# Two-layer conditioned decoder trunk: forming the first four conditioning pieces with TensorE, ahead of the layer that uses them

## The chip, the cores and the metric

The kernel runs on one core of one Trainium2 chip. The metric is the device time of one execution in microseconds; the kernel before and the changed kernel compute the same outputs from the same inputs.

## What is computed

Two layers, each a token mixer and a routed mixture of experts, on 512 tokens of 1024 features in f32. A vector `c` of 1024 numbers conditions each layer: `silu(c)` times a matrix of 1024 x 6144 plus a bias gives six rows of 1024, and the layer uses them as shift, scale and gate of its two halves.

```python
def reference(x, c, positions, w_ada, b_ada, ...):
    cond = jax.nn.silu(c)
    for l in range(DEPTH):                                    # DEPTH = 2
        mod = (cond @ w_ada[l] + b_ada[l])[:, None, :]        # 6 x 1024
        shift1, scale1, gate1, shift2, scale2, gate2 = jnp.split(mod, 6, axis=-1)
        h = _ada_norm(x, shift1, scale1)                      # rms(x) * (1 + scale1) + shift1
        x = x + gate1 * _token_mixer(h, positions, w_in[l], ...)
        h = _ada_norm(x, shift2, scale2)
        x = x + gate2 * _moe(h, w_router[l], ...)             # 64 experts, 8 per token
    return _rms_norm(x, final_gain)
```

`mod` is formed in twelve pieces of 512 columns. Pieces 0 and 1 are shift1, 2 and 3 are scale1: the first thing that a layer needs.

## The kernel before

`trunk` (from line 146) writes an opening block, a loop `Fori(0, DEPTH)` whose body is `mixer` and `experts`, each one block with a program for every engine and a barrier behind it, and a closing block with the last norm. Inside a block each engine runs its own list in the order in which it is written, held by semaphores. SP issues nearly all transfers, one after the other from one list, so a transfer is also held by every wait that stands before it in SP's list.

**Opening block (lines 196 to 245).** SP loads positions, the constants and x (2 MB). VectorE and ScalarE form the rotary tables (the last one at line 244), ScalarE the squares of x (line 238) and the root. TensorE has nothing there.

**Start of the mixer.** SP loads c, then eight blocks of 1 MB of `w_ada` (`ada`, line 388) and four short bias rows, then the input weights `w_in` in two parts (line 402: 1664 KB with the columns of queries and keys, then 3072 KB) and small weights. ScalarE applies silu to c (line 452). VectorE forms pieces 0 to 3 (lines 592 and 594): for each of eight chunks of 128 features it multiplies the 128 x 512 block by the chunk's column of c and adds, 32 operations. TensorE sums over the partitions with a matmul of ones (line 737), ScalarE copies the piece into `mod` (line 457). Then VectorE forms the normalised rows `h`, four tiles of 128 tokens, with lines 607 and 608; two tiles are in flight, and the third waits for TensorE's transposes (line 746) of the first.

The input projection works with split operands: every f32 operand is a rounded part ("hi") and a remainder ("lo"), and a product is three matmuls at the rate of the rounded type. So in front of it ScalarE rounds w_in chunk by chunk (line 461), GpSimd forms the remainders of the first part (line 437) after two small edits for the rotary columns (lines 433, 434), and VectorE forms those of the transposed rows (line 614) and of the second part (line 624). The rounded chunks 0 and 1 lie where `mod` keeps shift1 and scale1, so they come last, after line 608. TensorE's first product (line 753) waits for all eight remainders of GpSimd:

```python
pe.wait_ge(s_in_lo[0], DC)
pe.wait_ge(s_hT_hi, TJ)
```

The attention then runs head by head, and pieces 4 to 11 are formed beside it in the same way, one per head.

**Experts and combine.** Experts run in groups of three steps: two experts with split operands ("one") and a pair in plain f32 ("two"; lines 1719 and 1738). Each step gathers its tokens' rows and scatters its result to `y_rows` in HBM with indirect transfers that GpSimd issues (line 1241). SP's list brings the weights (lines 1130 to 1155). When all scatters have landed, SP reads `y_rows` back in 16 parts of 1 MB (line 1196, four buffers in `raw_gu`), VectorE adds them up tile by tile and adds the gated sum to x (lines 1592 to 1598), and ScalarE squares each finished tile (line 1365) and takes the root (line 1367) for the next norm. TensorE has nothing to do in the combine. The four tiles are one loop on each engine:

```python
for u in range(4 * TJ):
    wait(sp, s_ysum, u - 3)
    sp.dma_start(y_part[u % 4], y_rows[:, 2 * (u % 4):2 * (u % 4) + 2, u // 4, :]).then_inc(y_in[u % 4], 16)
```

## Time and profile before

| | |
|---|---|
| median of 3 runs | 2301.84 us (2300.92 to 2304.58) |
| the profiled execution | 2307.99 us, its span 2306.2 us |
| TensorE matmul busy | 1887.9 us, 82% of the span |
| VectorE busy | 1305.5 us, 57% |
| ScalarE, GpSimd busy | 914.2 us, 375.9 us |
| moved | 619.39 MB, mean 269 GB/s |
| mean granted TensorE clock | 0.891 |

The page gives busy time by engine and by group of instructions, with the idle time ahead of each and what ended it. A line number is a line of the kernel. PE is TensorE's matmul, PEld its loading of the stationary operand, DVE is VectorE, ACT ScalarE, POOL GpSimd, SP the engine that issues transfers; SPq is its queue. The two layers start their mixers at 22.58 and 1134.06 us.

### The profile page before, as it was taken

To read this page: it belongs to the slowest core of one execution; us is meant where nothing else is said; L and a number is where in the kernel's file an instruction comes from. 1 tells how busy PE (TensorE), PEld (TensorE's weight loads), DVE (VectorE), ACT (ScalarE), POOL (GpSimd) and SP (SyncE) were. 2 spreads that over 40 slices of the span, in tenths; PEclk is the share of its full clock that TensorE was granted. 3 is DMA by queue.
4 is the path that set the end of the run, shared out by engine and by line. 5 is a ranking of instruction groups with operands and counts; after the bars stand their busy time and mean duration, and the time that the engine had idled before them with its cause. 6 is when DMAs were issued, how large, how long until landed. Compare 5 with 4: busy or idle time off the path is not lost. (4 is left out here: it accounts for less than half of the span.)

```text
span 2306.2 us, 31250 instructions
## 1 busy us (share of the span) xinstructions
PE 1887.9 (82%) x8864; PEld 1313.8 (57%) x8865; DVE 1305.5 (57%) x1982; ACT 914.2 (40%) x1340; POOL 375.9 (16%) x281
## 2 busy tenths in 40 slices
PE   1888889889999899994068888988899989999960
PEld 0655677666666666662046456856666656666640
DVE  5647636555554546463774782556655554646447
ACT  2324521454544545451122342136454544545431
POOL 0200300122212222110020021002122212222110
PEclk9998889999989999997569779888899989999985
DMA  7035233689999999995632530556799999999956
GB/s 288 22 121 186 74 122 146 235 348 400 392 374 363 370 357 376 377 367 204 259 139 69 199 111 1 201 223 251 307 386 398 382 371 349 382 358 370 371 219 276
DMA packets 135180, 619.39 MB, mean 269 GB/s; under 512 B 22744, under 2 KB 25816, under 8 KB 81904
## 3 DMA queue, kind: packets, MB, share of 16 engines
q1 hardware_dynamic: 112240, 550.62, 62.8%
q0 software_dynamic: 22784, 67.13, 8.2%
q8 instruction: 44, 0.72, 0.1%
q14 instruction: 112, 0.92, 0.1%
HBM read 584.14 MB, written 46.14 MB: 273 GB/s over the span
## 5 line engine op out<-in xcount | busy, mean ns | idle before, releaser
L1526 DVE TENSOR_TENSOR w_lod<-raw_d,w_hid 128x2048 fp32r<-128x2048 f32 x72 | 165.4, 2297 | 263.2 <-ACT w_hid L1302 263.2
L1227 POOL DMA_INDIRECT mixT<-h_rows,gidx x104 | 144.9, 1393 | 787.4 <-issue 583.9
L1719 PE MATMUL bank<-hT,hbT 128*64 128x512 f32 x512 | 226.6, 595 | 0.0
L1719 PE MATMUL bank<-mod,hbT 128*64 128x512 f32 x512 | 226.6, 595 | 0.0
L1241 POOL DMA_INDIRECT y_rows<-mixT,sidx x104 | 144.5, 1390 | 459.8 <-issue 371.3
L1317 ACT ACTIVATE mixT<-bank 128x512 f32<-128x512 f32 x208 | 113.1, 600 | 208.2 <-PE bank L1738 116.3
L1685 PEld LDWEIGHTS bank<-meta,mod 128*128 128x128 f32 x1088 | 139.2, 198 | 66.8 <-issue 62.4
L1523 DVE TENSOR_TENSOR w_loa<-raw_gu,w_hia 128x2048 fp32r<-128x2048 f32 x72 | 164.8, 2290 | 19.8 <-ACT w_hia L1299 19.8
L1523 DVE TENSOR_TENSOR w_lob<-raw_gu,w_hib 128x2048 fp32r<-128x2048 f32 x72 | 164.4, 2283 | 0.0
L1342 ACT ACTIVATE mod<-bank 128x256 f32<-128x256 f32 x104 | 39.6, 381 | 309.5 <-PE bank L1698 178.0
L1685 PE MATMUL bank<-meta,mod 128*128 x1088 | 137.8, 254 | 29.8 <-DVE mod L1502 29.8
L1302 ACT ACTIVATE w_hid<-raw_d 128x2048 fp32r<-128x2048 f32 x72 | 138.1, 1917 | 37.3 <-DMA raw_d<-in_w_down 37.2
L1738 PE MATMUL bank<-h,actT 128*64 128x512 f32 x256 | 147.5, 730 | 5.4 <-ACT mixT L1317 5.4
L737 PE MATMUL bank<-acc,const 128*128 128x512 f32 x48 | 35.8, 838 | 141.1 <-DVE acc L594 141.1
L1299 ACT ACTIVATE w_hia<-raw_gu 128x2048 fp32r<-128x2048 f32 x72 | 137.6, 1911 | 29.6 <-PE bank L1698 29.5
L1692 PE MATMUL bank<-const,mixT 128*128 128x128 f32 x832 | 132.2, 309 | 20.6 <-POOLq L1235 20.5
L1696 PE MATMUL bank<-w_hia,hbT_r 128*128 128x512 f32 x288 | 124.3, 432 | 29.0 <-DVE hbT_lo L1531 25.6
L1738 PE MATMUL bank<-raw_d,actT 128*64 128x512 f32 x256 | 147.6, 730 | 0.0
L1719 PEld LDWEIGHTS bank<-hT,hbT 128*64 128x64 f32 x512 | 67.5, 137 | 131.8 <-issue 127.9
L1516 DVE COPY listed<-bank 128x3 f32 (+3 forms) x136 | 21.8, 160 | 205.2 <-PE bank L1685 204.1
L1299 ACT ACTIVATE w_hib<-raw_gu 128x2048 fp32r<-128x2048 f32 x72 | 137.9, 1915 | 0.0
L1692 PEld LDWEIGHTS bank<-const,mixT 128*128 128x128 f32 x832 | 118.1, 206 | 23.5 <-POOLq L1235 22.3
(347 smaller groups left out, 4228.4 us busy)
## 6 DMA issues: line engine op xcount, KB each, us to landing
raw_d<-in_w_down SPq DMA_DIRECT2D x104, 1024.0 KB, 11.1
raw_gu<-in_w_gate SPq DMA_DIRECT2D x72, 1024.0 KB, 10.9
raw_gu<-in_w_up SPq DMA_DIRECT2D x72, 1024.0 KB, 17.3
w_ada_sb<-in_w_ada SPq DMA_DIRECT2D x40, 1024.0 KB, 5.7
hT<-in_w_gate SPq DMA_DIRECT2D x32, 1024.0 KB, 7.9
hT<-in_w_up SPq DMA_DIRECT2D x32, 1024.0 KB, 13.3
mod<-in_w_gate SPq DMA_DIRECT2D x32, 1024.0 KB, 12.8
mod<-in_w_up SPq DMA_DIRECT2D x32, 1024.0 KB, 17.4
```

The lines of the kernel that those rows point to most:

```text
L1227: by_rows(s, lambda rows: pool.indirect_dma_start(out=hb[s.par][0:rows], out_offset=None, in_=h2_dram, in_offset=bass.IndirectOffsetOnAxis ...
L1241: by_rows(s, lambda rows: pool.indirect_dma_start(out=y_dram, in_=yb[s.par][0:rows], in_offset=None, out_offset=bass.IndirectOffsetOnAxis( ...
L1299: act.activation(w_hi[k][:].rearrange("p c g f -> p g c f"), raw_gu[s.side][:, :, 4 * k:4 * k + 4, :], ACT.Copy).then_inc(hi[k], 1)
L1302: act.activation(w_hi[2][:], raw_d[s.down_at][:], ACT.Copy).then_inc(hi[2], 1)
L1317: i = act.activation(yb[s.par][:, 512 * b:512 * b + 512], bank_y[b][:], ACT.Copy)
L1523: dve.tensor_tensor(w_lo[k][:].rearrange("p c g f -> p g c f"), raw_gu[s.side][:, :, 4 * k:4 * k + 4, :], w_hi[k][:].bitcast(F32).rearrang ...
L1526: dve.tensor_tensor(w_lo[2][:], raw_d[s.down_at][:], w_hi[2][:].bitcast(F32), ALU.subtract).then_inc(lo[2], 1)
L1685: i = pe.matmul(bank_l[:, 3 * k:3 * k + 3], sel[:, j, :], meta[:, j, bass.ds(e, 1), :].rearrange("p e k -> p (e k)"), start=j == 0, stop=j ...
L1692: i = pe.transpose(bank_t[c // 4][:, (c % 4) * P:(c % 4) * P + P], hb[s.par][:, c:D:DC], ident)
L1696: pe.matmul(dst, a_hi, b_hi, start=first, stop=False)
L1719: i = pe.matmul(bank_g[s.par][lane, :], hbT[:, c, lane], pair_gu[k][:, :, c, :], start=c == 0, stop=c == DC - 1)
L1738: i = pe.matmul(bank_y[b][lane, :], actT[:, c, lane], pair_d[k][:, c, 512 * b:512 * b + 512], start=c == 0, stop=c == 1)
```

## The change

- The opening block also loads c, the first layer's bias row (4 x 512) and its first 8 MB of w_ada, as four transfers of 2 MB (two chunks of 128 features, 2048 columns each) with x between the first and the second. ScalarE applies silu to c once into `cond`, which stays for the whole program.
- `first_pieces` lets TensorE do the whole product: the stationary operand is one column of `cond` repeated 128 times, the moving operand 512 columns of w_ada, so each output row is the product, and the result stands in all 128 partitions. Four banks hold pieces 0 to 3, eight chunks are summed in them, and the bias comes as a ninth product of a row of ones with the bias row: 36 matmuls in plain f32. `first_out` lets ScalarE copy the four banks to `mod`.
- The mixer no longer forms pieces 0 to 3. SP starts with w_in, VectorE with the normalisation.
- At the end of the experts of the first layer (`l < DEPTH - 1`, a branch on SP, ACT and PE) SP loads the next layer's first 8 MB of w_ada in eight pieces of 1 MB and the bias row, into weight buffers that the last steps leave free, each pair after the wait that says so; TensorE runs `first_pieces` behind its last down product, ScalarE `first_out` ahead of its squares of the combine.
- The parts of y_rows are read into the buffers of the split weights (`w_hi`, `w_lo`) instead of `raw_gu`.

The diff, cut to its core:

```diff
@@ trunk
+        cond = sb("cond", [P, DC])
...
+        def first_pieces(pe, w, row, arrived, done):
+
+            for c in range(DC):
+                pe.wait_ge(arrived[c], 16)
+                for q in range(4):
+                    pe.matmul(bank[q][:], cond[:, c:c + 1].to_broadcast([P, P]), w[c][:, q * 512:q * 512 + 512], start=c == 0, stop=False)
+            for q in range(4):
+                pe.matmul(bank[q][:], ones[0:1, :], row[:, q * 512:q * 512 + 512], start=False, stop=True).then_inc(done, 1)
+
+        def first_out(act, done):
+
+            for q in range(4):
+                act.wait_ge(done, q + 1)
+                i = act.activation(mod[:, q // 2, (q % 2) * 512:(q % 2) * 512 + 512], bank[q][:], ACT.Copy, bias=1.0 if q // 2 == SCALE1 else 0.0)
+            return i
...
                 sp.dma_start(const[:], ins["const"]).then_inc(s_start, 16)
-                sp.dma_start(x[:], x_in.rearrange("o (j p) n -> p (o j) n", p=P)).then_inc(s_x_in, 16)
+                sp.dma_start(raw_cond[:], c_in.rearrange("o (p c) -> p (o c)", c=DC)).then_inc(s_cond, 16)
+                sp.dma_start(first_row[:], ins["b_ada"][0:1, 0:4 * 512]).then_inc(d_first[0], 16)
+                src = ins["w_ada"][0:1].rearrange("o (p c) n -> p (o c) n", c=DC)
+                for i in range(4):
+                    sp.dma_start(first_w[:, 2 * i:2 * i + 2, :], src[:, 2 * i:2 * i + 2, 0:4 * 512]).then_inc(d_first[i], 16)
+                    if i == 0:
+                        sp.dma_start(x[:], x_in.rearrange("o (j p) n -> p (o j) n", p=P)).then_inc(s_x_in, 16)
...
+            @block.tensor
+            def _(pe):
+                pe.wait_ge(s_start, 32)
+                pe.wait_ge(s_cond, 17)
+                pe.wait_ge(d_first[0], 32)
+                first_pieces(pe, [first_w[:, c, :] for c in range(DC)], first_row, [d_first[c // 2] for c in range(DC)], s_first)
...
+                act.wait_ge(s_cond, 16)
+                act.activation(cond[:], raw_cond[:], ACT.Silu).then_inc(s_cond, 1)
...
                 act.wait_ge(s_start, 32 + 4 + 16)
+                first_out(act, s_first).then_inc(s_cond, 1)
+                act.wait_ge(s_cond, 18)
@@ mixer, SP
-                sp.dma_start(cond[:, 0, :], ins["c"].rearrange("o (p c) -> p (o c)", c=DC)).then_inc(d_small, 16)
-                ada(0)
-                sp.wait_ge(s_blank, 1)
-                for q in range(4):
-                    ada_row(q)
-                for u in range(1, 8):
-                    ada(u)
@@ mixer, ACT
-                for q in range(4):
-                    mod_out(q)
                 act.wait_ge(s_rot, 1)
-                act.wait_ge(s_unit, 8)
@@ mixer, DVE
-                for q in range(4):
-                    ada(q)
                 link(dve.reciprocal(stat[:, 8:12], stat[:, 20:24]))
-                dve.wait_ge(s_mod, 4)
@@ mixer, PE
-                for q in range(4):
-                    ada(q)
@@ experts
+        y_part = [plain[:].rearrange("p c g f -> p (c g f)").rearrange("p (k n) -> p k n", k=2) for plain, _ in both_hi + both_lo]
+        room = [raw_gu[0][:].rearrange("p g c f -> p (g c f)"), raw_gu[1][:].rearrange("p g c f -> p (g c f)"), hT[:].rearrange("p a n -> p (a n)")]
+        coming = [r[:, i * 2048:i * 2048 + 2048] for r in room for i in range(2)] + [plain[:].rearrange("p c n -> p (c n)") for plain in (hi_d, lo_d)]
+        coming_row = raw_d[0][0:1].rearrange("p a n -> p (a n)")
@@ experts, SP
+                last = group(GROUPS - 1, half + 1, 1)
+                with sp.If(l < DEPTH - 1):
...
+                    for i in range(2):
+                        sp.wait_ge(lo[1], last[i].order + 1)
+                        piece(2 * i)
+                        piece(2 * i + 1)
+                    sp.wait_ge(lo[2], last[1].order + 1)
+                    sp.dma_start(coming_row, ins["b_ada"][DEPTH - 1:DEPTH, 0:4 * 512]).then_inc(d_coming_row, 16)
+                    sp.wait_ge(s_gu, last[2].n + 1)
+                    piece(4)
+                    piece(5)
+                    sp.wait_ge(s_down, last[1].n + 1)
+                    piece(6)
+                    piece(7)
                 sp.wait_ge(s_scattered, (more + 3 * (GROUPS // 2)) * 2 + 2)
@@ experts, ACT
                 steps(act, step)
+                with act.If(l < DEPTH - 1):
+                    v["first_out"](act, s_first).then_inc(s_moved, 1)
+                    act.wait_ge(s_moved, 1)
@@ experts, PE
                 steps(pe, step)
+                with pe.If(l < DEPTH - 1):
+                    pe.wait_ge(d_coming_row, 16)
+                    v["first_pieces"](pe, coming, coming_row, d_coming, s_first)
```

How instructions move, as the two programs are built (a row is a line, an operation, what it writes from what, its shape and how many follow one another; the changed kernel's lines are numbered anew). First VectorE from the start of the mixer, before:

```order
L592 SCALAR_TENSOR_TENSOR acc<-w_ada_sb,cond,b_ada_rows 128x512
L594 SCALAR_TENSOR_TENSOR acc<-w_ada_sb,cond,acc 128x512 x7
L592 SCALAR_TENSOR_TENSOR acc<-hT,cond,b_ada_rows 128x512
L594 SCALAR_TENSOR_TENSOR acc<-hT,cond,acc 128x512 x7
L592 SCALAR_TENSOR_TENSOR acc<-mixT,cond,b_ada_rows 128x512
L594 SCALAR_TENSOR_TENSOR acc<-mixT,cond,acc 128x512 x7
L603 RECIPROCAL stat<-stat 128x4
L607 SCALAR_TENSOR_TENSOR h<-x,stat,mod 128x1024
```

and changed, where the normalisation is the first thing in the block:

```order
L586 UNCONDITIONAL_BRANCH
L615 RECIPROCAL stat<-stat 128x4
L618 SCALAR_TENSOR_TENSOR h<-x,stat,mod 128x1024
L619 TENSOR_TENSOR h<-h,mod 128x1024
L625 TENSOR_TENSOR hT_r<-bank,w_uq_sb_r 128x4x128
```

Then TensorE at the end of the experts' block in the changed kernel, where before the branch out of the block followed the last down product directly:

```order
L1776 MATMUL bank<-h,actT 64x512
L1776 MATMUL bank<-raw_d,actT 64x512
L1810 COMPARE_AND_BRANCH
L203 MATMUL bank<-raw_gu,cond 128x512 x16
L203 MATMUL bank<-hT,cond 128x512 x8
L203 MATMUL bank<-w_hid,cond 128x512 x4
L203 MATMUL bank<-w_lod,cond 128x512 x4
L205 MATMUL bank<-raw_d,const 128x512 x4
```

and SP at the same place, behind the last transfers of expert weights and ahead of the first read of y_rows:

```order
L1171 DMA raw_d<-in_w_down 128x2048
L1210 COMPARE_AND_BRANCH
L1214 DMA raw_gu<-in_w_ada 128x2048 x2
L1221 DMA raw_d<-in_b_ada 1x2048
L1214 DMA hT<-in_w_ada 128x2048 x2
L1214 DMA w_hid<-in_w_ada 128x2048
L1214 DMA w_lod<-in_w_ada 128x2048
L1231 DMA w_hia<-y_rows 128x2x1024
```

Nine transfers that were the next block's first now stand in this list between the weights and the parts of y_rows.

## Rows read from the trace of the kernel before

**Rows 1.** The page's groups of instructions: busy, mean ns, idle before, releaser.

```profile
L737 PE MATMUL bank<-acc,const 128*128 128x512 f32 x48 | 35.8, 838 | 141.1 <-DVE acc L594 141.1
```

**Rows 2.** Timeline of the first layer's start: start us, duration, instruction.

```profile
22.58 1.28 ACT L452 ACT_TABLE_LOAD   x1 [0.50 <-PEq L197]
...
23.17 0.41 SPq L388 DMA_DIRECT2D w_ada_sb<-in_w_ada  x1
...
28.45 0.75 DVE L592 SCALAR_TENSOR_TENSOR acc<-w_ada_sb,cond,b_ada_rows 128x512 f32<-128x512 f32 x1 [10.66 <-DMA w_ada_sb<-in_w_ada]
...
52.32 0.65 POOL L433 TENSOR_SCALAR w_in_sb<-w_in_sb 128x128 f32<-128x128 f32 x1 [27.64 <-DMA w_in_sb<-in_w_in]
52.92 0.82 POOL L434 COPY w_in_sb<-w_in_sb 128x128 f32<-128x128 f32 x1
...
57.05 1.50 ACT L461 ACTIVATE mod_r<-w_in_sb 128x448 fp32r<-128x448 f32 x3
57.25 1.28 DVE L607 SCALAR_TENSOR_TENSOR h<-x,stat,mod 128x1024 f32<-128x1024 f32 x1 [2.65 <-ACT mod L457]
57.70 5.98 POOL L437 TENSOR_TENSOR w_in_sb_r<-w_in_sb,mod_r 128x448 fp32r<-128x448 f32 x3 [3.95 <-ACT mod_r L461]
...
75.46 0.29 PEld L753 LDWEIGHTS bank<-w_uq_sb_r,mod_r 128*128 128x128 f32 x1 [1.59 <-POOL w_in_sb_r L437]
...
76.06 0.63 PE L753 MATMUL bank<-w_uq_sb_r,w_in_sb_r 128*128 128x512 f32 x1
...
81.18 0.49 PE L753 MATMUL bank<-w_uq_sb_r,w_in_sb_r 128*128 128x512 f32 x1
```

**Rows 3.** Timeline of the second layer's start.

```profile
1134.06 1.28 ACT L452 ACT_TABLE_LOAD   x1 [5.19 <-issue]
...
1134.86 1.40 SPq L388 DMA_DIRECT2D w_ada_sb<-in_w_ada  x1
...
1147.75 2.07 PE L737 MATMUL bank<-acc,const 128*128 128x512 f32 x2 [80.17 <-DVE acc L594]
...
1185.14 2.23 POOL L437 TENSOR_TENSOR w_in_sb_r<-w_in_sb,mod_r 128x448 fp32r<-128x448 f32 x2 [3.03 <-ACT mod_r L461]
...
1187.70 0.77 PE L753 MATMUL bank<-w_uq_sb_r,mod_r 128*128 128x512 f32 x1 [1.22 <-POOL w_in_sb_r L437]
...
1190.78 0.39 PE L753 MATMUL bank<-qk_r,w_in_sb_r 128*128 128x512 f32 x1
```

**Rows 4.** Stretches: us, busy PE, PEld, DVE, ACT, POOL, clock, DMA share, GB/s.

```profile
85.00:100.00 15.00, 15.00 (x66) 12.18 (x65) 4.15 (x6) 0.00 (x0) 0.00 (x0) 1.00 0.00 1
1154.00:1164.00 10.00, 4.15 (x4) 1.00 (x4) 9.54 (x13) 1.19 (x2) 0.00 (x0) 0.50 1.05 401
```

**Rows 5.** Timeline of the first layer's last steps and combine.

```profile
1073.53 39.03 SPq L1196 DMA_DIRECT2D raw_gu<-y_rows  x16
...
1062.27 0.39 PE L1747 MATMUL bank<-const,mod 128*128 128x128 f32 x2
...
1066.99 0.59 PE L1738 MATMUL bank<-raw_d,actT 128*64 128x512 f32 x1
...
1065.52 0.90 POOL L1241 DMA_INDIRECT y_rows<-mixT,sidx  x1 [9.53 <-issue]
1070.32 0.91 POOL L1241 DMA_INDIRECT y_rows<-mixT,sidx  x1 [3.90 <-issue]
...
1092.06 1.06 ACT L1365 ACTIVATE h<-x 128x1024 f32<-128x1024 f32 x1 [23.35 <-DVE x L1598]
...
1126.12 1.06 ACT L1365 ACTIVATE h<-x 128x1024 f32<-128x1024 f32 x1 [10.18 <-DVE x L1598]
```

**Rows 6.** Timeline of the opening block.

```profile
8.80 0.23 DVE L214 CAST identb<-const 128x128 bf16<-128x128 f32 x1 [8.68 <-DMA const<-in_const]
...
13.74 1.06 ACT L238 ACTIVATE mixT<-x 128x1024 f32<-128x1024 f32 x1 [3.61 <-DMA x<-in_x]
```

**Rows 7.** The values' product, the second layer: ns min, median, max; first and last start.

```profile
L841 PE MATMUL bank<-w_ukv_sb,latent x8: 592/592/667, 1255.1 to 1258.2; 128*128 128x512 f32 x8
```

81 lines of the change are left out of this document (41 added, 40 removed).

## The prediction

> **What bounds the kernel now.** I read the page's groups for the idle time first, then the timelines of the stretches that it points to, then engines and transfers by stretch, because the shares of the whole span hide it: TensorE is 82% busy over the span, and what this change touches lies in the stretches where it is not. The page's row of the conditioning matmul (line 737) carries 141.1 us of idle time in front of it, ended by VectorE's sum at line 594 [rows 1]; 80.2 of them are one wait at the start of the second layer that reaches back over the whole combine [rows 3]. So each layer opens with TensorE waiting for pieces 0 to 3, which VectorE forms one column block after another.
>
> The timeline of the first layer shows the chain [rows 2]. The mixer's block starts at 22.58. The first 1 MB block of w_ada is issued at 23.17 and used at 28.45. VectorE then works until the last piece is copied out, and ScalarE takes its next step at 57.05. In the same queue the input weights stand behind 8 MB of w_ada: GpSimd first touches them at 52.32. From there a second chain runs: two rotary edits on GpSimd (0.65 and 0.82 us), ScalarE's rounded copy of a chunk, GpSimd's remainder of it (57.70), eight of these, and TensorE's first projection product at 75.46. The second layer repeats it from 1134.06 to 1187.70 [rows 3]. Everything behind that first product depends on it alone, so I measure the change there: 52.9 us and 53.6 us after the block's start. The transfers fill those 50 us (share 1.05, 401 GB/s, [rows 4]), so the DMA engines would hold it too if VectorE were faster.
>
> The combine is the reverse: TensorE ends at 1067.6 and has nothing until the next layer, while VectorE adds the parts up to 1126.1, when ScalarE's last square follows it [rows 5]; the 16 MB of y_rows are loaded in the same time.
>
> **The opening block, first layer (term 1).** The diff takes 32 VectorE operations, 4 matmuls, 8 MB and the activation of c out of the mixer and puts 8 MB, 36 matmuls and 4 copies in front of it. The queue works in order: const is used at 8.80 and x, 2 MB, at 13.74 [rows 6], 4.9 us for 2 MB. With the activation's input and the bias row of some KB ahead, the first 2 MB of w_ada land at 14, x at 19, and the rest at 24, 29 and 34. Each pair carries 8 matmuls. A matmul on f32 with 512 columns is two instructions; eight of them from 1255.1 to 1258.2 are 0.44 us apart, 0.886 us a matmul at 2.4 GHz [rows 7]. At 1.2 GHz I take double the spacing: the one-pass products stand 0.43 us apart from 76.06 to 81.18 (twelve steps, up to 5.7 us after the first at 75.46) [rows 2] and 0.23 apart later (66 in 15 us) [rows 4]; hence 1.72 for a matmul. (The clock column says 1.00 for those slow us too, so I go by the spacing.) The first eight: 5.7 us slow (3.3 matmuls), 4.7 fast at 0.886, 4.2 us, done at 23.9. Then 28 at 0.886, 24.8 us, from 24 to 48.8, since data come faster than the 7.1 us a pair takes. Copy 0.6, block end 0.5 as before [rows 2]: the mixer starts at 49.9 instead of 22.58. The rotary tables and the squares of x end by about 28 and lie beside it.
>
> **From the block's start to the first product (term 2).** Now the first thing in the queue is the 1664 KB of w_in. A 1 MB block landed 4.87 us after its issue ended (23.58 to 28.45), the rest of the size adds 1.6 at 0.4 MB/us, the issue itself 0.45: 6.9. Rotary edits 1.42: 8.3. Copy and hand-over 0.65 (57.05 to 57.70): 9.0. Then eight remainders on GpSimd. In the trace three take 5.98 while VectorE runs lines 607 and 608, and two take 2.23 when it doesn't [rows 2, 3]. VectorE now starts its four rows of lines 607 and 608 at once, at 1.28 us the operation alone (57.25), 2.5 a row; with the wait for the transpose of the second row it is through at 10.5. So one remainder at 2.0 and seven at 1.12: 18.8, hand-over 0.29: **19.1**. ScalarE's order (six chunks, three turned rows at 1.1, two chunks) ends at 15.7, ahead of GpSimd. In the second layer the first issue with a register in its address took 1.40 instead of 0.41 [rows 2, 3], so 20.1 there. The bounds: every remainder at 1.12 saves 0.9; every one at 2.1, should VectorE keep in its way, costs 7 per layer. I take the mixed case since VectorE's later operands come from the banks, and the pair of 2.23 ran beside just those (line 614).
>
> First layer: product at 49.9 + 19.1 = 69.0 against 75.46, **6.5 gained**.
>
> **The combine, second layer (term 3).** In SP's queue the pieces stand behind the last weights; four of them go right after these, two when the last pair is multiplied and two after the second-last down product, near 1062.3 [rows 5], each step waiting for work that is done without them. TensorE goes on at 1067.6 at its high clock and needs 36 x 0.886 = 31.9 us: 1099.5; copied by 1100.1. ScalarE's first square, due at 1092.06 [rows 5], waits until then; the second is due a tile later, about 11 us by the 34 from the first to the last, so ScalarE has caught up by then. The cover is the combine, 26 us long from there. If that were gone, squares, table load and root (7.2 us) would follow the last copy.
>
> What isn't free is the DMA engines. Pieces 4 to 7, 4 MB, run from about 1061 to 1072 at 0.4 MB/us, and the last two scatters are issued at 1065.52 and 1070.32; y_rows may only be read when both have landed, at 1073.53 [rows 5]. The earlier scatter's half megabyte moves the pieces' end to 1072.7, so the last one shares the engines for part of its 2.3 us. Lower bound 0, if it finds them free; upper bound 2.6, one whole piece in front. I take 1.0, nearer to 0 as most of the pieces are through. The first read of y_rows and everything behind moves by that. The Trainium skill (DMA: Bandwidth & Descriptors, "Queues, rings and completion order") says that each DMA engine goes round-robin between the queue rows that have work, a packet at a time. By it a scatter runs at half rate while pieces are in flight, its 2.3 us become up to 4.6, and the sum would be 1.3 us less of a gain; no row here shows the two side by side at this place.
>
> So the second block starts at 1135.06 and the product comes at 1155.2 instead of 1187.7: 32.5. Against it, TensorE's clock: before, it went from 0.43 to 0.23 spacing 3.1 us after the first product (1187.70 to 1190.78) [rows 3], with four transposes shortly ahead; now there are 7 us of nothing ahead, and I take the first layer's 5.7. 2.6 us longer at half speed lose 1.3 (bounds 0 and 2.9). **31.2 gained**.
>
> Branches around the new code stand where the engine waits anyway. The second combine is as before, the attention's pieces 4 to 11 too.
>
> **Sum:** 6.5 + 31.2 = 37.7 us. The profiled execution took 2308.0 (span 2306.2), 6.2 above the median of the three runs; its stages need not be longer in the same places, so I subtract from the median: 2301.8 - 37.7 = **2264**.
>
> **Rivals.**
> A. *TensorE stays at 1.2 GHz through the opening.* Matmuls at 1.72 end at 14 + 13.8 + 48.2 = 76.0 instead of 48.8; the first layer loses 20.7 instead of gaining 6.5. Total 10.5 gained, 2291. For it: it stayed slow through every conditioning step of the second layer. Against: those were 2 us of work in 6.3, this is dense. 0.06.
> B. *Scatters queue behind pieces* as above, the full 2.6 or a little more: 2266. 0.10.
> C. *The stretch before the first product is longer*, GpSimd's remainders at 2.1 throughout, +14 over both layers: 2278. For it: six of eight ran so. 0.12.
> D. *The matmul is dearer than its rows*: the stationary operand is now one column of c repeated 128 times, loaded for each instruction, and it may neither overlap nor let the clock rise. With a price m per matmul the opening ends at 15.1 + 36m, and beyond m = 1.53 ScalarE's squares fall behind the combine (1067.6 + 36m + 7.2 against 1129.9). The total is 72m - 127.6: it loses from **m = 1.77** on. The isolated pair at line 737 took 2.07 [rows 3]: +21, slower, 2323. Against: nothing in the chain of 36 needs the one before but the bank's order, and four banks take turns. 0.05.
>
> The forecast itself has 0.67. 0.2% (4.6 us) is about what a measurement of this kernel can tell from no change; D with m between 1.71 and 1.84 would lie within it, 0.01 of its 0.05. All other cases are faster: faster 0.95, same 0.01, slower 0.04. The range holds the forecast with its bounds (2.9 of clock, 1.0 and 1.6 of scatters, 0.9 to some us of remainders, the runs' own 2 us), B and C: 2256 to 2280; A and D stay out.
>
> **What would show it.** Eight conditioning matmuls per layer of the old kind (lines 592 to 594 and 737) instead of twelve; the mixer's block starting near 50 and the first product near 69; in the second layer 20 us between them, the matmuls of line 203 in one run from 1068 to 1100 at 0.44 us spacing, the first read of y_rows issued within 2 us of 1073.5. Wrong it would be if the first product still waited for something after 25 us (then: who ends GpSimd's wait), or if ScalarE's last square came more than 2 us after VectorE's last addition.

## The result, and the profile after

The changed kernel takes 2269.99 us (median of 4 runs, 2267.44 to 2274.56) against 2301.38 for the kernel before (4 runs beside it, 2300.22 to 2304.58): ratio 0.9862, 95% interval 0.9839 to 0.9884, so 31.4 us faster. The forecast was 2264.0, a gain of 37.7. The profiled execution took 2274.56 us with a span of 2272.8 (before: 2307.99 and 2306.2). All medians here and below leave out two executions at a granted clock of 0.80 and 0.30, one of the kernel before (2382 us) and one of the changed kernel in run 2 (6172 us). Line numbers are those of the changed kernel from here on (in the rows of a run, those of that run's kernel): 203 and 205 are the conditioning products, 211 their copies, 460 GpSimd's remainders, 760 the first projection product, 1214 the pieces' loads, 1231 the reads of y_rows, 1276 the scatter, 1776 the last pair's down product.

The page's first part shows VectorE relieved by 57 us and TensorE busier by 50.5:

```profile
PE 1938.4 (85%) x8992; PEld 1339.1 (59%) x8993; DVE 1248.5 (55%) x1918; ACT 913.2 (40%) x1339; POOL 364.6 (16%) x281
```

**Opening block.** Timelines of TensorE, of ScalarE's last copy and of the mixer's first instruction on ScalarE (start us, duration, instruction):

```profile
14.08 9.16 PE L203 MATMUL bank<-first_w,cond 128*128 128x512 f32 x16 [14.08 <-DVE rotary L259]
23.75 20.87 PE L203 MATMUL bank<-first_w,cond 128*128 128x512 f32 x48 [0.50 <-DMA first_w<-in_w_ada]
44.54 3.69 PE L205 MATMUL bank<-first_row,const 1*128 1x512 f32 x8
...
48.27 0.60 ACT L211 ACTIVATE mod<-bank 128x512 f32<-128x512 f32 x1 [0.26 <-PE bank L205]
49.43 1.28 ACT L481 ACT_TABLE_LOAD   x1 [0.56 <-PEq L220]
```

The first 2 MB let TensorE start at 14.08. It waits 0.50 us for the second 2 MB, goes on without a pause from 23.75 (48 instructions in 20.87 us, 0.435 each, two to a product), and the mixer starts at 49.4, where 22.58 stood in [rows 2].

**Start of the first layer.** GpSimd's chain and the first product, which came at 75.46 in [rows 2]:

```profile
57.50 0.94 POOL L456 TENSOR_SCALAR w_in_sb<-w_in_sb 128x128 f32<-128x128 f32 x1 [6.02 <-DMA w_in_sb<-in_w_in]
58.39 1.30 POOL L457 COPY w_in_sb<-w_in_sb 128x128 f32<-128x128 f32 x1
60.38 3.32 POOL L460 TENSOR_TENSOR w_in_sb_r<-w_in_sb,mod_r 128x448 fp32r<-128x448 f32 x3 [0.70 <-ACT mod_r L481]
...
66.94 2.23 POOL L460 TENSOR_TENSOR w_in_sb_r<-w_in_sb,mod_r 128x448 fp32r<-128x448 f32 x2
...
69.22 0.80 PE L760 MATMUL bank<-w_uq_sb_r,mod_r 128*128 128x512 f32 x1 [7.66 <-POOL w_in_sb_r L460]
```

The remainders take 1.11 us each throughout, where three took 5.98 before [rows 2]. They no longer meet VectorE's norm, whose last operation ends at 59.54:

```profile
58.31 1.23 DVE L619 TENSOR_TENSOR h<-h,mod 128x1024 f32<-128x1024 f32 x1
```

**Combine and start of the second layer**, against [rows 3] and [rows 5]:

```profile
1046.33 1.80 SPq L1214 DMA_DIRECT2D raw_gu<-in_w_ada  x4
1061.31 1.94 SPq L1214 DMA_DIRECT2D hT<-in_w_ada  x2
1064.62 0.59 SPq L1214 DMA_DIRECT2D w_lod<-in_w_ada  x1
1076.72 0.39 SPq L1231 DMA_DIRECT2D w_hia<-y_rows  x1
...
1072.11 0.91 POOL L1276 DMA_INDIRECT y_rows<-mixT,sidx  x1 [3.90 <-issue]
...
1068.78 0.59 PE L1776 MATMUL bank<-raw_d,actT 128*64 128x512 f32 x1
1069.31 14.00 PE L203 MATMUL bank<-raw_gu,cond 128*128 128x512 f32 x32
1096.97 3.98 PE L205 MATMUL bank<-raw_d,const 1*128 1x512 f32 x8
1156.11 0.80 PE L760 MATMUL bank<-w_uq_sb_r,mod_r 128*128 128x512 f32 x1 [7.92 <-POOL w_in_sb_r L460]
...
1101.79 1.06 ACT L1403 ACTIVATE h<-x 128x1024 f32<-128x1024 f32 x1 [0.20 <-ACT mod L211]
1105.81 1.06 ACT L1403 ACTIVATE h<-x 128x1024 f32<-128x1024 f32 x1 [2.87 <-DVE x L1636]
1135.69 1.28 ACT L481 ACT_TABLE_LOAD   x1 [4.46 <-issue]
```

TensorE forms the pieces in one run under the combine (36 products from 1069.31 to 1100.95), ScalarE takes its first square 0.2 us behind the last copy and waits for VectorE again at the second, and the first product follows the block's start by 20.4 us instead of 53.6.

**Where the rest went.** The two stretches gained more than the whole. Stretches of the changed kernel, from the first projection product to the first gather of the experts, to the last pair's down product, to the next layer's first projection product, and so on (us, busy PE, PEld, DVE, ACT, POOL, clock, DMA share, GB/s):

```profile
69.20:379.20 310.00, 275.57 (x1238) 203.07 (x1239) 170.16 (x358) 91.67 (x206) 24.75 (x22) 0.88 0.30 106
379.20:1068.80 689.60, 633.39 (x3047) 429.93 (x3045) 367.84 (x514) 322.92 (x403) 136.78 (x99) 0.93 0.92 351
1068.80:1156.10 87.30, 40.02 (x108) 19.77 (x104) 59.45 (x54) 20.42 (x36) 13.17 (x13) 0.70 0.76 289
```

The same stretches of the kernel before:

```profile
75.50:384.90 309.40, 275.34 (x1239) 203.98 (x1240) 173.28 (x361) 92.91 (x208) 25.78 (x23) 0.89 0.30 106
384.90:1067.00 682.10, 625.60 (x3047) 423.41 (x3045) 367.56 (x514) 322.83 (x403) 138.32 (x99) 0.94 0.91 346
1067.00:1187.70 120.70, 16.77 (x44) 8.31 (x41) 86.45 (x83) 19.41 (x35) 18.79 (x13) 0.52 0.69 260
```

The opening to the first product went from 75.5 to 69.2 (6.3 gained), the stretch around the combine from 120.7 to 87.3 (33.4 gained), 39.7 in all. But the first layer's expert stage, with the same matmuls in it, went from 682.1 to 689.6: 7.8 us of TensorE's busy time more, at a granted clock of 0.93 instead of 0.94. That stage is what most of the experiments are about.

### The profile page after: what moved, and what is told of

Same layout as the page of the kernel before. It is cut to its first block and busy times, and to the rows that moved or that the text cites. A ratio compares the mean times of both kernels' runs of the same rounds, so it can differ in the third digit from the quotient of the medians.

```text
span 2272.8 us, 31364 instructions
## 1 busy us (share of the span) xinstructions
PE 1938.4 (85%) x8992; PEld 1339.1 (59%) x8993; DVE 1248.5 (55%) x1918; ACT 913.2 (40%) x1339; POOL 364.6 (16%) x281
## 5 line engine op out<-in xcount | busy, mean ns | idle before, releaser
L1564 DVE TENSOR_TENSOR w_lod_r<-raw_d,w_hid_r 128x2048 fp32r<-128x2048 f32 x72 | 165.5, 2298 | 270.2 <-ACT w_hid_r L1337 270.2
L1561 DVE TENSOR_TENSOR w_loa_r<-raw_gu,w_hia_r 128x2048 fp32r<-128x2048 f32 x72 | 164.8, 2289 | 18.2 <-ACT w_hia_r L1334 18.1
L1561 DVE TENSOR_TENSOR w_lob_r<-raw_gu,w_hib_r 128x2048 fp32r<-128x2048 f32 x72 | 164.3, 2282 | 0.0
L1377 ACT ACTIVATE mod<-bank 128x256 f32<-128x256 f32 x104 | 39.7, 382 | 307.1 <-PE bank L1736 175.5
L1337 ACT ACTIVATE w_hid_r<-raw_d 128x2048 fp32r<-128x2048 f32 x72 | 138.0, 1916 | 39.3 <-DMA raw_d<-in_w_down 39.3
L1730 PE MATMUL bank<-const,mixT 128*128 128x128 f32 x832 | 133.1, 310 | 19.8 <-POOLq L1270 19.8
L1334 ACT ACTIVATE w_hia_r<-raw_gu 128x2048 fp32r<-128x2048 f32 x72 | 137.6, 1911 | 26.0 <-PE bank L1736 25.9
L1734 PE MATMUL bank<-w_hia_r,hbT_r 128*128 128x512 f32 x288 | 123.7, 430 | 28.3 <-DVE hbT_lo L1569 24.9
L1334 ACT ACTIVATE w_hib_r<-raw_gu 128x2048 fp32r<-128x2048 f32 x72 | 137.8, 1914 | 0.0
L1734 PE MATMUL bank<-w_hid_r,actT_r 128*128 128x512 f32 x288 | 126.1, 438 | 7.8 <-issue 7.8
```

Source lines behind the costliest of these rows:

```text
L1334: act.activation(w_hi[k][:].rearrange("p c g f -> p g c f"), raw_gu[s.side][:, :, 4 * k:4 * k + 4, :], ACT.Copy).then_inc(hi[k], 1)
L1337: act.activation(w_hi[2][:], raw_d[s.down_at][:], ACT.Copy).then_inc(hi[2], 1)
L1561: dve.tensor_tensor(w_lo[k][:].rearrange("p c g f -> p g c f"), raw_gu[s.side][:, :, 4 * k:4 * k + 4, :], w_hi[k][:].bitcast(F32).rearrang ...
L1564: dve.tensor_tensor(w_lo[2][:], raw_d[s.down_at][:], w_hi[2][:].bitcast(F32), ALU.subtract).then_inc(lo[2], 1)
L1730: i = pe.transpose(bank_t[c // 4][:, (c % 4) * P:(c % 4) * P + P], hb[s.par][:, c:D:DC], ident)
L1734: pe.matmul(dst, a_hi, b_hi, start=first, stop=False)
```

## The experiments

The edits below are shortened: `...` and lines in words stand for code that is left out.

Two theories at first: **W**, the expert stages wander by several us from execution to execution, and the gain of the medians only looks small; **S**, the change makes them longer. A third, **L**, came after the first four runs.

**1 and 2. Both kernels again**, without an edit.

> The kernel before, once more. The expert stage of layer 1, first gather to the end of the last pair's down product, took 682.1 us in the profiled run of before (384.88 to 1066.99) and 689.5 us in that of the changed kernel (379.25 to 1068.78), with the same instructions in it. The theory that this stage wanders from run to run (theory W) expects this profile to show another length, somewhere in 680 to 692 us, and all else of the kernel to within 1 us of the first profile. The theory that the change itself makes the stage longer (theory S) expects 682 to 683 us again.

> The changed kernel, once more. Theory W (the expert stages wander by several us with the granted clock and the phase of the loads): a length of layer 1's expert stage somewhere in 680 to 692 us, not tied to 689, and with five rounds a ratio to the kernel before nearer 0.984 (37 us) than the 0.9862 of the first result. Theory S (the change makes the stage longer by some 7 us): 689 to 690 us again and a ratio of 0.986. By both the opening ends at 49.4, layer 1's first projection product comes at 69.2, and the stretch from the last down product of layer 1 to layer 2's first projection product is 87.3 us (120.7 before).

Measured: the kernel before 2303.72 (12 runs) and 2302.23 (22 runs beside it), with single executions from 2293 to 2314; the changed kernel 2268.56 (5), ratio 0.9864, interval 0.9834 to 0.9894. First-layer experts: 686.3 us before, 685.4 after. So the stage does wander by 4 us (W), in both kernels; S's fixed 682 and 689 are out. W had also expected a ratio nearer to 0.984. It came out at 0.986 again, but the interval holds both values, so these two runs alone don't show that a part of the gain is missing.

**3. The place: the second layer's pieces on TensorE at the mixer's start**

```
 mixer, SP queue, before w_in:
+    with sp.If(l > 0):
+        sp.wait_ge(s_blank, 1)
+        sp.dma_start(raw_row, b_ada[0:4 * 512]); for c in range(DC): piece(c)   # the eight loads
 mixer, tensor engine, before the transposes:
+    with pe.If(l > 0): first_pieces(...)
 expert stage:
-    the eight loads, first_pieces and first_out beside the combine
```

ScalarE copies the pieces out as its first step in the mixer, and VectorE's norm waits for the copies.

> Layer 2's pieces are formed by the tensor engine as in the changed kernel, but at the start of the mixer, with its loads first in the mixer's queue, and not beside the combine. The opening is the changed kernel's. If the gain in layer 2 comes from the place (the combine leaves the tensor engine and the queue free), almost all of it goes: 8 MB take some 25 us to land, the tensor engine ends about 40 us after the block starts, and the first projection product follows 18 to 20 us later, so 58 to 60 us after the block starts, against 53.6 in the kernel before and 20.4 in the changed one. The combine gets back about 1.5 us. That makes some 36 us more than the changed kernel, 2303 to 2308 us, slower than the kernel before or level with it. If the rival holds, that the tensor engine instead of the vector engine is what gains, the product comes about 30 us after the block starts and the time is near 2280 us.

Measured: 2311.39 us (10 runs; 2303 to 2308 expected), ratio 1.0038 (1.0021 to 1.0056), slower than the kernel before. Timelines of ScalarE's first instruction in the second mixer, and of TensorE:

```profile
1127.84 1.28 ACT L211 ACT_TABLE_LOAD   x1 [4.60 <-issue]
...
1134.64 10.11 PE L203 MATMUL bank<-w_ada_sb,cond 128*128 128x512 f32 x16 [72.07 <-DMA w_ada_sb<-in_w_ada]
1165.28 4.54 PE L205 MATMUL bank<-b_ada_rows,const 1*128 1x512 f32 x8
1188.95 0.77 PE L777 MATMUL bank<-w_uq_sb_r,mod_r 128*128 128x512 f32 x1 [1.22 <-POOL w_in_sb_r L470]
```

The first product comes 61.1 us after the block's start (58 to 60 expected, 53.6 before, 20.4 in the changed kernel). TensorE forms the pieces in 35.2 us (1134.64 to 1169.82), VectorE took 28.8 for them in the first layer (28.45 to 57.25, [rows 2]); the 6.4 us between the two are most of the 7.5 by which the product is later. About 3 of them are TensorE's lower clock at the start: the first 16 instructions take 10.11 us with 0.50 granted until 1140, the next 16 take 7.03. The engine gains nothing, it loses. The place under the combine gains 40 us by the stretch (126.9 against 87.3 and 86.7) and 43 by the medians (2311.4 against 2268.6). No run has the opening's part alone.

**4. The pieces' last 4 MB behind the first reads of y_rows**

```
-    sp.wait_ge(s_gu, ...); piece(4); piece(5); sp.wait_ge(s_down, ...); piece(6); piece(7)
     for u in range(4 * TJ):
+        if u == 4:
+            with sp.If(l < DEPTH - 1): piece(4) ... piece(7)
```

> Of layer 2's eight rows of weights, the last four (4 MB) are not loaded ahead of the reads of the expert outputs but after the first four of the 32 reads. The theory that the scatters and the first reads are slowed by the pieces' 4 MB (put at 1.0 us in the prediction, 1.4 us in the first profile of the changed kernel) expects the first read within 0.5 us of the kernel before, 3.2 us after scatter and last product rather than 3.2 plus 1.4 later; 4 MB at the 330 GB/s of the combine then stretch the 32 reads by up to 12 us where the combine is bound by them, by 3 to 6 us where its adds are. The root then ends 2 to 8 us later than in the changed kernel, and the whole is 2 to 8 us slower. If the combine were bound by adds throughout, nothing would be lost and 1 us gained.

Measured: 2277.53 us (2 runs, 14 us apart), ratio 0.989 (0.9843 to 0.9936); the stretch around the combine takes 94.7 us instead of 87.3, 7.4 more (2 to 8 expected for the whole). SP's queue:

```profile
1074.62 0.41 SPq L1229 DMA_DIRECT2D w_hia<-y_rows  x1
1075.07 0.46 SPq L1229 DMA_DIRECT2D w_hib<-y_rows  x1
1075.58 0.47 SPq L1229 DMA_DIRECT2D w_loa<-y_rows  x1
1076.09 0.83 SPq L1229 DMA_DIRECT2D w_lob<-y_rows  x1
1077.37 0.84 SPq L1214 DMA_DIRECT2D hT<-in_w_ada  x2
```

The last down product started at 1068.10, so the first read comes 6.52 us behind it: 6.54 in the kernel before (1066.99 to 1073.53, [rows 5]), 7.94 in the changed one (1068.78 to 1076.72). So the 4 MB beside the scatters put the first read off, and taking them away gives that back. How much it is varies: the first read comes 6.52 to 6.56 us behind the last down product in the five profiles without these loads (before, 1, 6, 3, 4), and 7.05 to 7.94, mean 7.51, in the nine with them. That is **1.0 us**, 0.5 to 1.4 in single profiles. The loads pay for themselves: behind the first reads they hold up the next ones, and VectorE waits 7.4 us at 1099.95 for a part:

```profile
1091.32 1.22 DVE L1634 TENSOR_TENSOR x<-x,mixT 128x1024 f32<-128x1024 f32 x1
1099.95 1.23 DVE L1628 TENSOR_TENSOR mixT<-w_hia 128x1024 f32<-128x1024 f32 x1 [7.40 <-DMA w_hia<-y_rows]
```

**Theory L.** After these four I compared the medians with the two stretches. They take 195.6 us in the kernel before, 156.2 in the changed one and 196.4 in run 3 (means of the profiles there were); with 1.8 us outside the span, the rest of the kernel takes 2104.9, 2110.6 and 2113.2 of the medians beside run 3 (2104.0 and 2112.0 by the first measurement). So 6 to 8 us are missing in both kernels that have the opening's part, wherever the second layer's pieces are formed. What these two share beside the opening is a detail of the diff: the vector `cond`, 32 bytes a partition, moved out of the mixer to a place ahead of every tile of both layers. The mixer's and the expert stage's first tile starts at byte 114048 of a partition before, a multiple of 128, and at 114080 after; all tiles of the expert stage follow. (In the mixer those behind the vector's old place, 64 bytes wide, start 32 bytes lower than before.)

**5 and 10. The 32 bytes made 128**

```
-        cond = sb("cond", [P, DC])
+        cond = sb("cond", [P, 4 * DC])[:, 0:DC]
```

> The changed kernel with one tile wider: the conditioning vector takes 128 bytes of each partition instead of 32. Nothing else differs. In the kernel before, the first tile of the mixer and of the expert stage starts at byte 114048 of a partition, a multiple of 128; the change puts its 32-byte vector ahead of it, and every later tile of both layers starts 32 bytes further on, at 114080. Theory L says that this shift is what takes back the missing gain: outside the two stretches that the change works on (opening to first projection product, last down product to next projection product) the medians leave 2104.9 us for the kernel before and 2112.4 for the changed one, so 7 to 8 us. It expects 2262 to 2265 us here, ratio to before 0.983. Theory W (no cost of the change at all, only scatter from run to run) and the theory that the cost comes from the later phase of the loads expect 2270 to 2271 us, ratio 0.986, as with the 32-byte vector.

> The changed kernel with the conditioning vector in a tile of 128 bytes, again, now on the same chip as the changed kernel itself. The first time it stood at 0.9846 of before, 0.0018 under the changed kernel, with intervals that overlap; the kernel before with all tiles moved by 32 bytes stood at 1.0009, whose interval excludes the 7 us of theory L and leaves at most 5. If the 32 bytes cost anything, this run is 3 to 5 us under the changed kernel again; if not, within 1.5 us of it.

**6. The kernel before with its tiles moved by 32 bytes**

```
         stat = sb("stat", [P, 32])
+        sb("shift", [P, DC])
```

> The kernel before with an unused tile of 32 bytes a partition behind the small statistics tile, so that all tiles of the mixer and of the expert stage start 32 bytes further on, as in the changed kernel. Theory L expects 2309 to 2310 us, 7 to 8 more than before (ratio 1.003); the others expect no change, 2302 us (ratio 1.000).

**9. The changed kernel a third time**, no edit.

> The changed kernel a third time, beside the three that follow. The two measurements so far gave ratios of 0.9862 and 0.9864 (31 us) where its stretches sum to 39 us of gain in the profiles. If the missing part is a cost of the change, the ratio is 0.986 again; if it is scatter between executions, it may be anywhere from 0.983 to 0.987.

Measured:

```
                                  median (runs)   beside: before   ratio   95% interval
 5 changed, 128 bytes             2267.34 (4)     2305.43          0.9846  0.9824 to 0.9868
10 changed, 128 bytes             2262.23 (6)     2302.44          0.9821  0.9789 to 0.9854
 9 changed                        2270.52 (6)     2302.44          0.9849  0.9813 to 0.9885
 6 before, moved by 32 bytes      2306.47 (12)    2305.43          1.0009  0.9995 to 1.0022
```

Run 5 missed what L expected of it, 2262 to 2265 us and 0.983: its interval holds L's ratio and the other theories' 0.986. Runs 9 and 10 share a chip, and there the wider tile stands 8.3 us under the changed kernel, more than the 3 to 5 expected. Runs 11 and 12 (below) are a second pair that differs in nothing else: 9.4 us. Of each pair the means of six executions are 2269.8 and 2262.5, and 2264.0 and 2255.7; one execution scatters by 4 to 6 us, so one difference is uncertain by some 3 (standard error), and both together are 7.7 with 2.2. The pair is shown then, if not its size. But the kernel before, moved by the same 32 bytes, lost 1.0 us, at most 5 by its interval: L's second half (2309 to 2310) failed. Its tiles of the expert stage stand at the same bytes as in the changed kernel. The two agree only at 3 to 5 us, or if something else of the changed kernel makes it sensitive. Which, I can't say.

The profiles point to a stage. Lengths in us, one profile each, from each run's own instruction rows:

```
                              to 1st    to        experts  to 2nd    to        experts  to
                              product   gather    layer 1  product   gather    layer 2  end
before                        75.5      309.4     682.1    120.7     309.1     735.3    74.1
 1 before again               76.0      313.1     686.3    118.9     307.9     732.8    73.9
 6 before, moved              76.3      309.6     681.7    119.7     307.8     729.2    73.7
changed                       69.2      310.0     689.6     87.3     308.8     733.7    74.2
 2 changed again              69.1      308.0     685.4     86.7     306.2     733.1    74.0
 9 changed, third             70.9      309.9     689.8     86.4     304.8     735.5    74.1
 3 place                      69.5      306.5     686.0    126.9     306.3     734.2    74.2
 4 late pieces                69.2      310.0     688.9     94.7     308.9     736.9    74.4
 7 shared opening             67.0      308.4     684.7     87.0     306.0     736.1    73.9
 8 products ahead             70.7      306.9     685.2     86.2     301.6     734.9    74.1
11 both additions             64.7      308.4     692.4     87.1     306.2     732.0    73.8
 5 128 bytes                  69.3      309.3     682.8     86.4     309.3     733.2    73.9
10 128 bytes again            68.1      308.3     682.0     85.9     307.2     734.4    73.7
12 both, 128 bytes            65.0      305.6     685.3     86.7     306.2     732.8    74.2
```

The first layer's expert stage has a mean of 683.4 us in the three profiles of the kernel before (one of them run 6, with 681.7 in spite of its moved tiles), 687.8 in the eight with the 32-byte tile, 683.4 in the three with 128. Of the stretches that no edit touches, only the second layer's experts have a mean that rises too, from 732.4 to 734.6 (733.5 with 128 bytes), which is within their scatter; both stretches to the gather have means 2 us shorter. And the profiles of the two kernels themselves don't show the missing part: outside the two stretches the kernel before leaves 2112.0 us (two profiles) and the changed kernel 2112.4 (three). The profiled executions of the kernel before lie 7 us above its medians, those of the changed kernel 1. So where the loss of the medians lies is a reading, not shown. Within the stage a difference goes together with TensorE's granted clock. From the fourth to the fifth ten-microsecond stretch behind the first gather, in the changed kernel:

```profile
409.20:419.20 10.00, 8.60 (x34) 6.98 (x34) 4.96 (x10) 0.77 (x2) 2.99 (x1) 0.83 0.88 331
419.20:429.20 10.00, 7.09 (x24) 5.78 (x26) 0.45 (x2) 1.62 (x4) 0.97 (x1) 0.66 1.02 421
```

and in run 10:

```profile
406.40:416.40 10.00, 8.54 (x32) 6.96 (x32) 4.28 (x8) 0.74 (x2) 2.99 (x1) 0.76 0.94 377
416.40:426.40 10.00, 8.36 (x36) 5.84 (x38) 0.00 (x0) 3.96 (x6) 1.06 (x2) 0.83 1.00 404
```

24 instructions against 36 in the same 10 us, at 0.66 against 0.83. The fifth gather comes 59.8 us behind the first in the changed kernel (59.8 in run 9, 57.3 in run 2) and 57.4 in run 10 (57.4 in 5 and 12), 57.3 in the kernel before (59.8 in run 1, 57.3 in 6). Of the other five runs with the 32-byte tile three have 59.3 to 59.8 (3, 4, 11) and two 57.3 and 57.4 (7, 8). So there are two courses that this stage takes, some 2.5 us apart by its fifth gather, and either kernel shows both. They divide the fourteen profiles without exception: the stage takes 681.7 to 685.4 us in the eight of the short course and 686.0 to 692.4 in the six of the long one. The long one came in one of three profiles of the kernel before, five of eight with the 32-byte tile and none of three with 128, and so few profiles can fall that way by chance. Whether the bytes make the long course likelier, and by what, no run tells.

**7. Part of the opening to VectorE**

```
+  vector engine:  first_acc = sum over c in range(DC) of first_w[:, c, 3 * 512:] * cond[:, c]
   tensor engine:
+  for q in range(4): matmul(bank[q], ones[0:1, :], first_row[q], start=True)       # rows first
   for c in range(DC):
-      for q in range(4): ...
+      for q in range(3): ...
+  matmul(bank[3][:], ones, first_acc[:], stop=True)
```

> The changed kernel with a quarter of the opening's work moved off the tensor engine: the vector engine, idle there, forms piece 3 of layer 1 by eight multiply-adds, and the tensor engine sums it over the partitions by one product at the end; the bias rows come first. If the opening is bound by the tensor engine at its lower clock level for most of its length (as the first profile of the changed kernel shows: 48 products in 20.9 us at 0.43 each), 8 of 32 products less make the mixer start at 41 to 43 us instead of 49.4, and the whole 6.5 to 8 us faster than the changed kernel, near 2263 us. If the loads bound it (the last of them lands at about 34 us), the mixer would start at 45 or later and the gain be under 4 us.

Measured: 2266.72 us (4 runs; near 2263 expected), ratio 0.9849 (0.9827 to 0.9872). The mixer starts at 47.2, not at 41 to 43. (The expectation called 0.43 us an instruction the lower clock level. That was wrong: two instructions make a product, and 0.43 each is the higher level, 0.86 the lower.) TensorE's timeline:

```profile
14.10 7.16 PE L278 MATMUL bank<-first_row,const 1*128 1x512 f32 x8 [14.10 <-DMA first_w<-in_w_ada]
21.19 23.94 PE L282 MATMUL bank<-first_w,cond 128*128 128x512 f32 x48
44.96 1.02 PE L286 MATMUL bank<-first_acc,const 128*128 128x512 f32 x2
```

The eight one-row instructions (one partition of operands) take 0.86 us each, and so do the first eight behind them; its weight loads show the step to 0.43 spacing at 27.3. In the changed kernel, which begins with 128-partition products at 14.08, that step comes at 18.4. Seven us of one-row products went by without the higher level, and that took most of what the shorter work gave. The expectation's other case, that the loads hold the opening, would also have put the mixer at 45 or later; it is out, because the 48 instructions run without a wait for a load.

**8. Ten products ahead of each layer's first one**

```
+                pe.wait_ge(s_in_lo[0], 1); pe.wait_ge(s_hT, 1)
+                for n in range(10): pe.matmul(bank[0][...], w_in_hi[...], w_in_r[...], start=True, stop=True)
                 pe.wait_ge(s_in_lo[0], DC)
```

> The changed kernel with ten products more in each layer, whose result is thrown away (they write a bank that the first real product starts anew), placed where the tensor engine waits for the vector engine's rounded inputs before the first projection product. In the changed kernel's profile products run at the lower clock level for some 5.3 us after layer 2's first one (1156.11 to 1161.40), and gain nothing of their own. If the clock rises by earlier work, these stretches shrink and each layer gains up to half of 5.3 us: 2 to 5 us in all, 2266 to 2268 us. If it doesn't, or if the added products delay the first real one, 2270 to 2273 us.

Measured: 2268.65 us (4 runs; 2266 to 2268 expected), ratio 0.9862 (0.9836 to 0.9888): no gain that can be told. The mechanism is there, in TensorE's timeline of the second layer:

```profile
1144.76 4.07 PE L791 MATMUL bank<-w_in_sb_r,mod_r 128*128 128x448 f32 x10 [3.50 <-DVE hT_r L625]
1149.00 0.67 PE L760 MATMUL bank<-w_uq_sb_r,mod_r 128*128 128x512 f32 x1 [0.16 <-POOL w_in_sb_r L460]
1149.51 0.40 PE L760 MATMUL bank<-w_uq_sb_r,w_in_sb_r 128*128 128x512 f32 x1
1149.74 0.39 PE L760 MATMUL bank<-w_uq_sb_r,mod_r 128*128 128x512 f32 x1
```

The spacing is 0.23 from the second product on, where the changed kernel had 0.43 until 1161.40, 5.3 us long. Twelve products in 3.1 us instead of 5.3 are 2.2 us, and 1.6 in the first layer (2.9 instead of 4.5). That is less than four runs resolve whose executions lie 17 us apart, and in this profile the opening took 1.4 us back (mixer at 50.8). The first product isn't later for the ten: what ended the wait is still GpSimd.

**11 and 12. Both additions, with 32 and with 128 bytes.** As 7 and 8, but the weights first, and the one-row products between the second and the third row of weights, where TensorE waits for a load:

```
   for c in range(DC):
+      if c == 2:
+          for q in range(4): matmul(bank[q], ones[0:1, :], first_row[q], start=q == 3, stop=False)
```

> The changed kernel with both additions: the vector engine forms piece 3 of layer 1 in the opening, the tensor engine starts with the weights at once and puts the four one-row products of the bias between the second and the third row of weights, where it waits for a load; and ten products ahead of each layer's first projection product. In the run with the shared opening one-row products came first, and the higher clock level came at 27.3 instead of 18.1; here it should come at 18 as in the changed kernel, so that the opening's products end at 41 instead of 48.2 and the mixer starts at 42 to 43.5. The first product of layer 1 then follows at 62 to 63.5 (69.2), at the higher level. With 2 to 3 us in each layer from the added products that makes 9 to 12 us less than the changed kernel: 2259 to 2262 us where that takes 2271. If the clock stays low with the one-row products in between, the mixer starts at 47 or later and the gain is 3 to 5 us.

> The same kernel with the conditioning vector in 128 bytes. A second pair for the 32 bytes: if they cost anything this is 3 to 5 us under the run with both additions, if not within 1.5 us.

Measured: 2263.59 us (ratio 0.9825, 0.9789 to 0.9860) with 32 bytes and **2254.15 us (0.9789, 0.9756 to 0.9823)** with 128: 48 us under the kernel before, 16 under the changed one beside it. The opening of run 11:

```profile
14.16 7.72 PE L283 MATMUL bank<-first_w,cond 128*128 128x512 f32 x12 [14.16 <-DVE rotary L261]
21.82 3.70 PE L280 MATMUL bank<-first_row,const 1*128 1x512 f32 x8
25.44 17.41 PE L283 MATMUL bank<-first_w,cond 128*128 128x512 f32 x36
44.91 1.28 ACT L502 ACT_TABLE_LOAD   x1 [0.56 <-PEq L222]
```

and a row of its stretches, 25 to 29 us:

```profile
25.00:29.00 4.00, 4.00 (x7) 1.50 (x6) 0.58 (x2) 2.19 (x3) 0.00 (x0) 0.59 1.01 426
```

The mixer starts at 44.9, 4.5 us earlier than in the changed kernel; 42 to 43.5 was expected. The missing 2 are the clock again: behind 3.7 us of one-row products the granted clock falls to 0.59 (0.66 in run 12) and 36 instructions take 17.41 us instead of 15.5, in both runs. Run 11 gains 6.9 us on run 9 (9 to 12 expected); its first-layer experts took 692.4, the longest of all. Of the 16 us of run 12, 9.4 are the pair's difference, where 3 to 5 was expected.

## Why the prediction was right, and where it was off

The gain, its sign and the range held; the point was 6.0 us low.

- *Opening block (term 1).* The first 2 MB at 14, as read from [rows 6]; products at 0.87 us (0.886); the mixer at 49.4 (49.9; 49.3 and 51.1 in runs 2 and 9). The low level held for 4.3 us instead of 5.7, but that gave nothing, because TensorE then waited for the second 2 MB. These came at 23.75 instead of 24, and 28 products took 24.5 us instead of 24.8: that is the half microsecond. Rival A is out: 48 instructions in 20.87 us.
- *Block to first product (term 2).* 19.8 us (19.1), and that it came so near is luck, because its parts were off against each other. GpSimd first used w_in 8.1 us after the block's start, where the sum had 6.9. The rotary edits took 0.94 and 1.30 instead of 0.65 and 0.82, beside VectorE's norm. So the first remainder came at 10.95 instead of 9.0. By then the norm was over (10.1 after the block's start), so that no remainder ran at 2.0 and all at 1.11: 8.8 us to the first product, where the sum had 9.8 and 0.29. Rival C is out for that reason. In the second layer the same: first use at 9.5 (7.9), first remainder at 11.6 (10.0), product at 20.4 (20.1).
- *The first layer's gain.* 6.3 (6.5); 6.0 by the means of two and three profiles.
- *Combine (term 3).* 36 products in 31.6 us (31.9), copied by 1101.6, 0.2 ahead of ScalarE's first square, which was caught up by the second. Rival D is out: m was 0.88. The scatters put the first read off by 1.4 us here and by 1.0 on the mean of nine profiles, which is my 1.0; rival B's 2.6 is out. (The sign "within 2 us of 1073.5" did not hold as written: the read came at 1076.72, since the last down product was itself 1.8 later.) By the rule of the Trainium skill (DMA: Bandwidth & Descriptors, "Queues, rings and completion order"), a round-robin between queues, I had put it at 2.3 with all of the last scatter under the pieces; by the time alone the rule may hold for a part of that scatter, but no row tells how the packets were mixed.
- *From down product to product.* 33.4 us gained in the first pair of profiles, 33.0 by the means of two and three; 32.5 was forecast for this stretch. The profile that I worked from had its first addition 12.3 us behind the last down product, where four others without the loads ahead of the reads had 11.3 to 11.5; so the base was nearly 1 us too long. The 1.3 us that the sum took off again for the clock lie behind the product, in the next stretch: the slow part there was 5.3 us (5.7).
- *The sum.* For the two stretches the forecast had 39.0 (6.5 and 32.5), and the profiles show 39.0 by those means. The medians show 31.4, 33.7 and 31.9 in three measurements. Their ratios taken together are 0.986, 0.9844 to 0.9876 (an estimate, from the three intervals as independent): 28 to 36 us, so a part of the 37.7 is missing. **What failed is a term that the sum put at nothing:** that every stage between the two stretches keeps its length. What took its place is shown only in part. With the 128-byte tile the medians are 38.1 and 40.2 us under the kernel before, around the forecast's 37.7 and the stretches' 39.0. The profiles of the first layer's expert stage, 30% of the kernel, point there (about 4 us longer with the 32-byte tile, and not with 128), but the kernel before with its tiles moved has 681.7.
- *The base.* I subtracted from the median rather than from the profiled execution, which was 6.2 above it; the repeats confirm 2302 to 2305 as the kernel's level. Most executions of one kernel lie within 10 us of it (one was 18 above), so a single profile of each would have "shown" 33.4 here, 46.4 in runs 1 and 2 (2310.66 and 2264.26).

Open stay: why the same 32 bytes cost the kernel before little or nothing; what in the expert stage they act on; and where the rest of the missing gain lies (39.0 less 31.4 to 33.7 is 5 to 8, the expert stage's part 4.4 at most).

## What to carry to other kernels

Sum a change by the stretches it touches, and then check that the stretches it doesn't touch kept their length over several profiles; a small tile that moves ahead of all others is part of the change, and it is cheap to try it at 128 bytes. What gains here is the place: work that TensorE does no faster than VectorE is worth 40 us under a stage that leaves TensorE idle, and less than nothing at the start of the layer. Products that only bridge a wait of TensorE can bring its clock up, but here that stayed below what a measurement tells, and one-row products were followed by the lower level.

## What the runs showed of the hardware that I had not expected

- Products with one partition of operands went ahead of a fall of TensorE's clock, and of a late rise. Eight instructions of them at the start ran 0.86 us apiece, as did the next eight instructions of 128 partitions, and the higher level came at 27.3 instead of 18.4 (run 7 against the changed kernel). 3.7 us of them in the middle were followed by 0.59 for 4 us (run 11). At the opening's end they ran in 3.69 to 3.75 us in six of eight profiles, but took 5.02 in run 9 and 4.98 in run 8. That the one partition is the reason is not shown: no run has the same instructions with 128 partitions in that place.
- The recorded clock reads 1.00 for the first 20 us, while products there stood 0.86 us apart until 18.4; only their spacing tells the level.
- GpSimd and VectorE were both slower beside each other. In the kernel before, VectorE's line 607 took 2.16 us while GpSimd's remainders ran (1.99 each), and 1.28 alone; in the changed kernel GpSimd's copy of the second rotary edit took 1.30 us beside the norm and 0.28 in the second layer, where the norm had just ended (1146.30 against 1146.19). The rows:

```profile
60.53 2.16 DVE L607 SCALAR_TENSOR_TENSOR h<-x,stat,mod 128x1024 f32<-128x1024 f32 x1
```

```profile
1146.30 0.28 POOL L457 COPY w_in_sb<-w_in_sb 128x128 f32<-128x128 f32 x1
```

- Executions of one kernel on one core, minutes apart, differ by 10 us and more (2293 to 2314), and the expert stage's length goes with TensorE's granted clock in it.
